# The first unit's up and down slots are refilled in quarters, and down products take chunks outside, column halves inside

## The reference

```
h = h + mix @ w_o[l]                       # after two groups of attention heads
h = h + hier_moe(rms_norm(h, norm2_g[l]), ...)
...
# hier_moe: 4 groups of 8 experts; each token takes one group and two experts in it
for gi in range(N_GROUPS):
    h = silu(einsum('nd,edf->nef', xt, w_gate[gi])) * einsum('nd,edf->nef', xt, w_up[gi])
    y = y + einsum('nef,efd->nd', h * combine[:, gi, :, None], w_down[gi])
```

## Time and profile before

| | before |
|---|---|
| median of 3 runs | 605.11 us (604.78 to 606.01) |
| the profiled execution: its own time / its span | 604.16 us / 602.3 us |
| mean granted TensorE clock | 0.936 |
| TensorE matmul busy | 514.4 us (85%) |
| VectorE / ScalarE busy | 132.3 us (22%) / 71.0 us (12%) |
| ring and other DMA, MB over the span | 217.56 MB, mean 361 GB/s |

### The profile page before, as it was taken

The page is one execution under the profiler, slowest core; times in us unless marked ns, Lnnn a source line. Parts: engine busy times, 40 slices in busy tenths (PEclk is TensorE's granted clock), DMA queues, the critical chain, the costliest instruction groups (busy, mean ns, idle before and its releaser), DMA issues.

```text
span 602.3 us, 6699 instructions
## 1 busy us (share of the span) xinstructions
PE 514.4 (85%) x2681; PEld 240.9 (40%) x2681; DVE 132.3 (22%) x308; ACT 71.0 (12%) x140; POOL 28.2 (5%) x58
## 2 busy tenths in 40 slices
PE   4999799978999999999999999999959553855294
PEld 2445577546444453535353535353514110411031
DVE  1005565334102020303030303030303000300023
ACT  2013324131010101010101000000100000000002
POOL 2032020040000000000000000000000000000001
PEclk9999999986999999999999999999989856986699
DMA  6898491152889999999999999999999999999991
GB/s 251 326 385 365 175 383 13 36 207 108 299 344 432 425 423 430 429 428 429 430 428 429 427 429 430 429 428 427 425 431 427 428 424 431 429 425 429 414 373 72
DMA packets 23944, 217.56 MB, mean 361 GB/s; under 512 B 5041, under 2 KB 6089, under 8 KB 12401
## 3 DMA queue, kind: packets, MB, share of 16 engines
q1 hardware_dynamic: 19680, 214.31, 85.3%
q10 hardware_dynamic: 4240, 2.94, 1.6%
HBM read 216.18 MB, written 1.06 MB: 361 GB/s over the span
## 4 chain that ended last, share of the span: by engine, by line
PE 71%; DMA 22%; SPq 3%; DVE 2%; issue 1%; ACT 0%; POOL 0%; DVEq 0%; POOLq 0%; ACTq 0%
PE bank L1206 27%; PE bank L1221 13%; PE bank L1178 7%; DMA ring<-in_w_down_dram 7%; PE bank L1241 6%; DMA ring<-in_w_gate_dram 5%; DMA ring<-in_w_up_dram 5%; PE bank L1073 5%; PE bank L1004 4%; DMA ring<-bias_line 3%; PE bank L1063 2%; SPq L366 2%; PE bank L1041 1%; PE bank L1052 1%; PE bank L987 1%
## 5 line engine op out<-in xcount | busy, mean ns | idle before, releaser
L1206 PE MATMUL bank<-ring,region_x 128*64 128x512 f32 (+1 forms) x1024 | 191.9, 636 | 50.6 <-DMA ring<-in_w_up_dram 27.6
L1206 PEld LDWEIGHTS bank<-ring,region_x 128*64 128x64 f32 (+1 forms) x1024 | 60.8, 134 | 178.7 <-issue 178.7
L1221 PE MATMUL bank<-ring,region_q 128*64 128x512 f32 (+1 forms) x512 | 95.7, 624 | 7.0 <-DMA ring<-in_w_down_dram 5.7
L874 DVE TENSOR_TENSOR region_q<-region_q,bank 128x512 f32<-128x512 f32 x13 | 8.9, 687 | 312.5 <-PE bank L1206 312.5
L1221 PEld LDWEIGHTS bank<-ring,region_q 128*64 128x64 f32 (+1 forms) x512 | 29.7, 131 | 63.8 <-issue 61.4
L1178 PE MATMUL bank<-region_q,region_t 128*128 128x128 f32 x416 | 51.1, 284 | 1.8 <-DVE region_q L861 1.8
L1241 PE MATMUL bank<-region_x,region_q 128*128 128x512 f32 x104 | 50.6, 618 | 0.7 <-ACT region_x L606 0.7
L1178 PEld LDWEIGHTS bank<-region_q,region_t 128*128 128x128 f32 x416 | 50.1, 200 | 1.8 <-issue 1.8
L1004 PE MATMUL bank<-ring,region_x 128*128 128x512 f32 x96 | 42.6, 596 | 2.2 <-DMA ring<-in_w_in_dram 1.4
L880 DVE TENSOR_TENSOR h<-h,bank 128x512 f32<-128x512 f32 x52 | 35.7, 687 | 21.9 <-PE bank L1241 21.9
L606 ACT ACTIVATE region_x<-bank 128x512 f32<-128x512 f32 x26 | 15.5, 597 | 135.0 <-PE bank L1221 135.0
(11 more groups left out here) (172 smaller groups left out, 248.5 us busy)
## 6 DMA issues: line engine op xcount, KB each, us to landing
ring<-in_w_gate_dram SPq DMA_DIRECT2D x32, 2048.0 KB, 18.4
ring<-in_w_up_dram SPq DMA_DIRECT2D x31, 2048.0 KB, 16.1
ring<-in_w_down_dram SPq DMA_DIRECT2D x27, 2048.0 KB, 18.1
ring<-in_w_down_dram SPq DMA_DIRECT2D x20, 512.0 KB, 13.8
ring<-in_w_in_dram SPq DMA_DIRECT2D x8, 768.0 KB, 9.4
ring<-in_w_o_dram SPq DMA_DIRECT2D x2, 2048.0 KB, 8.6
ring<-in_w_up_dram SPq DMA_DIRECT2D x4, 512.0 KB, 5.6
ring<-bias_line ACTq DMA_DIRECT2D x1, 1536.0 KB, 15.4
```

The costliest lines, as they stand in the source:

```text
L874: dve.tensor_tensor(act_sb, silu_sb, ps[UP][:], ALU.mult).then_inc(act_done, 1)
L1206: last = pe.matmul(ps[bank][rows, :], xgT[:, c, rows], slots[fill_slot(f + a)][:, c * F:(c + 1) * F], start=(c == 0), stop=(c == KC - 1))
L1221: last = pe.matmul(ps[GD0 + half][rows, :], hT[:, c, rows], slots[fill_slot(f + a)][:, c * D + 512 * half:c * D + 512 * half + 512], start ...
```

## The change

After the eight quarters of slots 5 and 6, which stay, SyncE refills slots 7 and 8 (down of expert 3 for unit 1, first gate of unit 2) in quarters while the up products of unit 0 run (`up_pieces`), and slots 0 and 1 (second gate and first up of unit 2) in quarters while down(0) runs (`down_pieces`). So that quarters of a down matrix come free early, `down` takes its four chunks as the outer loop and the two column halves as the inner one, in every unit, and waits for both `xg_act` and `xg_dve` ahead of its first matmul. The expert order for unit 2 is read after the first of the new quarters. In the loop's second step, which is run three times, TensorE also waits for the first three quarters of the new fills ahead of down and ahead of the gate products.

```diff
             for c in range(PIECES):
                 if c < PIECES - 1:
                     sp.wait_ge(gate_pieces, c + 1)
                 else:
                     sp.wait_ge(gate_done, 1)
...
-            wait_used(fill_at(1, 2, 1))
-            load(1, 2, 1, 3)
-
-            sp.wait_ge(order_ready, 1)
-            for u in range(2, UNITS):
+                load_quarter(fill_at(1, 1, 1), c, up_e[3][:, quarter(c)], first_pieces_in)
+                load_quarter(fill_at(1, 2, 0), c, down_e[2][:, quarter(c)], first_pieces_in)
+            for c in range(PIECES):
+                if c < PIECES - 1:
+                    sp.wait_ge(up_pieces, c + 1)
+                else:
+                    sp.wait_ge(up_done, 1)
+                load_quarter(fill_at(1, 2, 1), c, down_e[3][:, quarter(c)], second_pieces_in)
+                if c == 0:
+                    sp.wait_ge(order_ready, 1)
+                    experts = order_of(2)
+                load_quarter(fill_at(2, 0, 0), c, chosen_quarter(gate_e, experts[0], c), second_pieces_in)
+            for c in range(PIECES):
+                if c < PIECES - 1:
+                    sp.wait_ge(down_pieces, c + 1)
+                else:
+                    sp.wait_ge(down_done, 2)
+                load_quarter(fill_at(2, 0, 1), c, chosen_quarter(gate_e, experts[1], c), third_pieces_in)
+                load_quarter(fill_at(2, 1, 0), c, chosen_quarter(up_e, experts[0], c), third_pieces_in)
+            wait_used(fill_at(2, 1, 1))
+            load(2, 1, 1, experts[1])
+            for a in range(2):
+                wait_used(fill_at(2, 2, a))
+                load(2, 2, a, experts[a])
+
+            for u in range(3, UNITS):
...
-                for half in range(2):
-                    pe.wait_ge((xg_act, xg_dve)[half], after + 1)
-                    for c in range(FC):
+                pe.wait_ge(xg_act, after + 1)
+                pe.wait_ge(xg_dve, after + 1)
+                for c in range(FC):
+                    for half in range(2):
                         last = down_chunk(n_e, f, half, c)
-                    last.then_inc(down_done, 1)
+                        if c == FC - 1:
+                            last.then_inc(down_done, 1)
+                    if c < FC - 1:
+                        last.then_inc(down_pieces, 1)
...
-            products(0, 2, 0, fill_at(0, 1, 0), UP, up_done)
+            products(0, 2, 0, fill_at(0, 1, 0), UP, up_done, up_pieces)
...
+                if j == 1:
+                    pe.wait_ge(second_pieces_in, 16 * 2 * (PIECES - 1))
                 down(before, n_before, base, f_before, i)
+                if j == 1:
+                    pe.wait_ge(third_pieces_in, 16 * 2 * (PIECES - 1))
                 products(i, n_e, base, f, GATE, gate_done)
```

More of the change, by code:

```diff
@@ L266, in build_encoder @@
         w_in_in = [sem(f"w_in_in{c}") for c in range(KC)]
-        gate_pieces, first_pieces_in = sem("gate_pieces"), sem("first_pieces_in")
+        gate_pieces, up_pieces, down_pieces = map(sem, ("gate_pieces", "up_pieces", "down_pieces"))
+        first_pieces_in, second_pieces_in, third_pieces_in = map(sem, ("first_pieces_in", "second_pieces_in", "third_pieces_in"))
         last_in = [sem(f"last_down_in{c}") for c in range(FC)]
@@ L340, in _, with quarter, load_quarter, chosen_quarter @@
             load(1, 1, 0, 2)
-            up_slot, down_slot = slots[fill_slot(fill_at(1, 1, 1))], slots[fill_slot(fill_at(1, 2, 0))]
+            def quarter(c):
+                return slice(c * SLOT // PIECES, (c + 1) * SLOT // PIECES)
+            def load_quarter(f, c, source, early_in):
+                s = fill_slot(f)
+                sp.dma_start(slots[s][:, quarter(c)], source).then_inc(early_in if c < PIECES - 1 else slot_in[s], 16)
+            def chosen_quarter(src, expert, c):
+                return src[bass.ds(expert, 1), :, quarter(c)].rearrange("a p n -> (a p) n")
+            def order_of(u):
+                e0 = first_expert(u)
+                return [sp.value_load(expert_at[0:1, e0 + a:e0 + a + 1], min_val=0, max_val=EXPERTS - 1) for a in range(ways(u))]
             for c in range(PIECES):
@@ L346, in _ @@
                     sp.wait_ge(gate_done, 1)
[L347 to L350, removed]
-            wait_used(fill_at(1, 2, 1))
-            load(1, 2, 1, 3)
-            sp.wait_ge(order_ready, 1)
-            for u in range(2, UNITS):
-                e0 = first_expert(u)
-                experts = [sp.value_load(expert_at[0:1, e0 + a:e0 + a + 1], min_val=0, max_val=EXPERTS - 1) for a in range(ways(u))]
+                load_quarter(fill_at(1, 1, 1), c, up_e[3][:, quarter(c)], first_pieces_in)
[23 more added lines that the diff above has]
+            for u in range(3, UNITS):
+                experts = order_of(u)
                 for m in range(3 if u < UNITS - 1 else 2):
```

## The result

The changed kernel is slower. Median 608.36 us against 605.89 us for the kernel before, 20 runs each; ratio 1.0056 with a 95% interval of 1.0034 to 1.0078, so 2.1 to 4.7 us. I had forecast 0.7 us slower (605.8 us, range 604.0 to 607.8), within what a measurement can tell from no change. Of the 2.6 us between 605.8 and 608.36, 0.8 is the base, which had a median of 605.11 in three runs and has one of 605.89 in twenty; the change itself costs 2.5 us where 0.7 was forecast. All ratios compare runs in the fast state, which leaves out one of e7's twelve (610.03 us).

A forecast was written before the change was run, and what follows sets the result against it. DMA was taken to set the end. Holes -5.6, quarters +2.2, queue empty at down(1) +3.2 and lateness by down(9) +0.9 summed to +0.7 us: 605.11 becomes 605.8 us, range 604.0 to 607.8.

The forecast's parts named there:

- What bounds the kernel: From 180 us to the tail: DMA sets the end at 424 to 432 GB/s; a gain must come before 180 us.
- The quarters: Refills at 162 to 180 us: 5.6 us of holes go, 2.2 us lost to lower rate, slots full 3.4 us sooner.
- The queue is never empty here: During up(0) and down(0): freed quarters keep DMA supplied, so 5.6 us of holes go.
- 0.24 us: At the fill released by down(1): what is left of the 3.4 us gained, landing at 213.91 instead of 214.15.
- The delay of a step: At the first down matmul of every unit: waiting for the VectorE copy costs 0.68 us a step.
- What exceeds 7.8 is the slack in this release: At each down's first fill: landing time beyond 7.8 us is slack, 1.6 us at down(1) growing to 6.1.
- 6.1 us of slack: At down(9): its fill landed 13.9 us after issue against 7.8; 6.80 us of delay makes it 0.7 us late.
- a queue that nearly runs dry in each unit may lose a little each time: In each unit's DMA queue: an argument for the slower rival, with no size given.
- The weighed rule: Fill on an empty queue: the skill page gives an estimated 6.8 us landing, sum 0.3 us faster; the row's 7.8 decides.
- The slower one: First down matmul of ten steps: delay of 0.88 us, +2.7 us, 607.8 us; chance 0.35.
- its threshold of 0.73 us: First down matmul: the delay a step from which the slower rival decides, (6.1 + 1.2) / 10.
- The faster one: At down: copy wait under 0.2 us a step, down(1)'s 1.6 us slack limits, 1.6 us faster, 603.5 us; chance 0.09.

The follow-up runs named there:

- e7: Changed kernel with the VectorE copy wait behind the first two down matmuls, plus quarter refills of slots 6 and 7 during down(1): ratio 0.9962 against before.
- e2: Changed kernel with the VectorE copy wait moved behind the first two down matmuls: ratio 0.9985 against before, step 28.83 us.
- e3: Kernel before with only the VectorE copy wait moved ahead of the first down matmul, halves still outside, whole fills: ratio 1.0056, step 29.56 us.
- e1: Kernel before with the changed down loop alone (chunks outside, both waits first), without the new quarter refills: ratio 1.0035 against before.
- e6: e1 with a useless half-size VectorE copy ahead of the one down waits for: step 29.89 us, 1.06 longer than before.
- e4: Changed kernel with a useless second full-size VectorE copy ahead of the one down waits for: step 30.15 us, 1.32 longer than before.
- e5: e1 with the VectorE copy wait between the first and second down matmul: step 29.46 us, 0.63 longer than before.
- e10: Kernel before, whole fills, with chunks outside and the VectorE copy wait behind the first two down matmuls: ratio 1.001, step 28.83 us.
- e9: e7 with TensorE's unit loop written out and quarter refills behind down(1), (2), (3) and (4): ratio 1.000 against before.

## Why the prediction was wrong

**What bounds the kernel: right.** DMA sets the end, with TensorE's releases limiting it up to unit 10. The changed kernel's progress is lost up to about 440 us and then stays 2.3 to 2.7 us behind, as the chain shows: TensorE up to 446.74, then a landing.

**The quarters: right in kind, somewhat mis-sized.** I forecast 5.6 us of holes against 2.2 us of lower rate, a lead of 3.4 us; measured at 204.6 us it is 2.5, of which TensorE's later down(0) takes about half a microsecond (3.0 in e2). "The queue is never empty here" didn't hold: the first quarter that down(0) releases lands 3.6 us after its issue, as one on an empty queue does (3.2 to 3.6 in the runs), and a window there moves 340 GB/s. At down(1) all of the lead is lost in the changed kernel. I had left 0.24 us. The landing of its fill bears that out (65.9 us from the first gate product, 66.1 before), but the bytes are 0.7 us behind. What the quarters bring in the end is 0.4 us at most.

**The delay of a step: slightly mis-sized.** I took 0.68 us and measured 0.73: TensorE starts 0.15 us after the copy's end and not 0.10. Ten steps make that 0.5 us. I had named 0.73 as the point from which slower decides.

**The step that failed: "What exceeds 7.8 is the slack in this release."** I took the landing on an empty queue, 7.8 us, as a sharp limit above which nothing is lost, and set ten delays, 6.80 us in all, against 6.1 us of slack. With the true delay the same sum gives 7.3 - 6.1 = 1.2 us; measured is 2.7 to 2.8 in the changed kernel and 2.6 to 3.2 in e3 and e1. The missing 1.5 us or so is lost while the queue is nearly empty but not dry: the windows at 240, 330 and 360 us (388, 366, 350 GB/s) and the 12 us around each release (407 to 423 GB/s) show it in the changed kernel, and e6 and e4, where the queue does run dry, come back near the sharp limit (4.2 and 7.5 us against 4.5 and 7.1). I had named this ("a queue that nearly runs dry in each unit may lose a little each time") and given it no price. As an estimate fitted to the runs, a release is free only while its fill would land more than 9 to 9.5 us after issue. That takes 1.2 to 1.7 us off each slack: 7.3 - (6.1 - 1.5) = 2.7 us, and 6.3 - 4.6 = 1.7 for e5 (1.5 measured). It isn't a formula for larger delays: for e6 it would say 6.0, where 4.2 to 5.1 was measured.

**The weighed rule.** By the fixed part and rate of the Trainium skill, "DMA: Bandwidth & Descriptors", section "Anatomy of one DMA — SWDGE (gpsimd) path", the landing would be an estimated 6.8 us and the kernel 0.3 us faster. The runs don't agree: they show 7.5 to 8.0 us for a whole fill on a dry queue. The row was the nearer, and even that was too low as a limit.

**The rivals.** The slower one came true in its effect and partly in its mechanism: the delay reached its threshold of 0.73 us, without coming near 0.88. That its price of 2.7 us is close to the 2.5 to 2.8 measured is luck, for it was worked out for 0.88 and the sharp limit. The faster one has its counterpart in e2: without the delay the kernel isn't slower, but the lead is cut to 0.4 us in progress, not to 1.6. The range ended at 607.8, 0.6 us short of the median of 608.36.

Settled by the runs: the loss is the moved wait (e1, e3 against e2, e10). Not settled: what in the DMA engines makes a nearly empty queue slower, and whether the quarters alone bring anything.

## What to carry to other kernels

When a loop is turned inside out, look where its waits end up: a wait that came 3.5 us into the products for nothing became 0.73 us of idling in each of ten steps, and a wait behind the first two matmuls costs nothing (step 28.83 us in e2 and e10). In a ring that is limited by transfers, the slack of a release is its landing time less that of a fill on an empty queue, but here the last 1 to 2 us of it weren't free. A lead won at the start of this ring lasted only to the first release that depends on the compute engine, so look for that release before counting the holes as a gain.

## What I had not expected of the hardware

A wait between two matmuls that work on different columns of the array costs nearly as much as one ahead of both: 0.63 us a step in e5 where 0.3 was planned and 0.73 is the full wait. With less than about one fill of 2.1 MB left in it, the queue moved 350 to 399 GB/s in the 3 us around the next release, where it moved 428 with more. And eight quarters of 512 KB cost 0.3 us behind down(1), and about 0.5 us a block in e9, where the first sixteen cost 2.6 us (5.6 us of holes less a lead of 3.0), with the queue nearly empty for part of them.
